# FFN input products of a two-block FP32 kernel as Strassen's seven block products, with the sums of weight blocks on GpSimd

## The chip, the cores and the metric

The kernel runs on one core of one Trainium2 chip. The metric is the device time of one launch in microseconds. Matrix products run on TensorE (PE in the profile; PEld is its weight load), the rest on VectorE (DVE), ScalarE (ACT) and GpSimd (POOL); SyncE (SP) issues the loads.

## The reference, cut to what matters

512 tokens of width 1024 pass a first block (gated linear attention, then an FFN) and a second one (FFN, pool and retention mixer, FFN), all in float32. The three FFNs have the width 2816 and are what the change touches:

```python
def swiglu_2(x, w1, w3, w2):
    return (jax.nn.silu(x @ w1) * (x @ w3)) @ w2
...
    h = h + 0.5 * swiglu_2(rmsnorm(h, ffn1_norm[l]), ffn1_w1[l], ffn1_w3[l], ffn1_w2[l])
```

`x @ w1` is called the gate here, `x @ w3` the up product, their gated product the hidden values (22 chunks of 128).

## The kernel before, in words

Activations are feature-major: a tile `[128, k, 512]` holds 128 features by 512 tokens for each k. Every float32 operand of a large product is two parts, an upper one rounded to the matmul's type (`hi`) and the rest (`lo`), and `mm3` makes three matmuls of each product: hi by hi, hi by lo, lo by hi. Each loads its own weights.

SP loads weights in units of 1 MB (1024 features by 256 columns) into `w_raw[0]` and `w_raw[1]`. ACT rounds a unit to `w_hi` (L1265), DVE subtracts it from the raw one into `w_lo` (L1712, one instruction of 2048 elements), and PE uses both. The FFN's first stage is `group`: a unit of gate columns into banks 0 and 1, a unit of up columns into banks 2 and 3, 96 matmuls of 512 tokens. ACT takes silu of the gate, DVE multiplies gate and up and splits the hidden value at once into `g_hi` and `g_lo` (L2282 or L2292, and L2297). 11 groups make an FFN's first stage; the first is written apart, ten are a loop. FFN 1 and 2 multiply their results by the norm's roots on DVE (`scaled`); FFN 0 does not. The second stage, `out_body`, runs over four column units in four parts each (`OUT_PARTS`).

Engines are in order, each with its own instruction list, and meet by semaphores alone; the order is written by hand. GpSimd has root computations (L420), sums of squares (L434, L436), residual adds (L458) and the pool mixer.

## Time and profile before

| | us |
|---|---|
| median of 3 runs | 1609.38 (1608.78 to 1611.98) |
| span of the profiled execution | 1607.1 |
| PE busy | 1596.4 |
| DVE busy | 849.0 |
| ACT busy | 502.5 |
| POOL busy | 119.9 |

The profiled execution has no own time beside its span: the profile gives the span from the first instruction to the last, and the median of the runs is 2.3 us above it. Busy is the union of an engine's instructions; matmuls overlap in their pipeline, so PE's pace is read from the distance of their starts.

### The profile page before, as it was taken

Reading aid. Unit: us, or ns where it says so; the run is one execution under the profiler, and the core shown is the slowest. Engines: PE = TensorE matmul, PEld = TensorE weight load, DVE = VectorE, ACT = ScalarE, POOL = GpSimd, SP = SyncE. Lnnn points to the kernel's source line nnn. Section 1 sums busy time; section 2 is a strip of 40 time slices with the busy share of each in tenths; the row PEclk is TensorE's granted clock in tenths of the full one; section 3 lists DMA queues with packets and bytes.
Section 4 is the critical chain, followed back from the end, with each engine's and each line's share of the span. In section 5 each row is a group of like instructions: output and inputs, shape, how many; then the busy total and the mean of one; then the engine's idle time right before and its main releaser. Section 6 shows DMA issues by size and latency. Waiting matters only on the chain.

```text
span 1607.1 us, 19314 instructions
## 1 busy us (share of the span) xinstructions
PE 1596.4 (99%) x7785; PEld 1343.6 (84%) x7785; DVE 849.0 (53%) x1050; ACT 502.5 (31%) x589; POOL 119.9 (7%) x106
## 2 busy tenths in 40 slices
PE   9999999999999999999999999999999999999998
PEld 7888888888888888888888888888988888888887
DVE  5898764664433344584454444346456544444444
ACT  4554375522222233442222223221323222222222
POOL 0100000020000000000000003135006000000000
PEclk9999999999999999999999999999999999999999
DMA  9544511222222123322222223342212322222332
GB/s 388 193 156 159 208 53 53 80 79 96 87 104 104 66 89 98 116 79 105 99 84 104 91 73 105 98 146 103 80 53 79 105 104 94 89 104 69 95 100 77
DMA packets 30647, 171.35 MB, mean 107 GB/s; under 512 B 3200, under 2 KB 5504, under 8 KB 17152
## 3 DMA queue, kind: packets, MB, share of 16 engines
q1 hardware_dynamic: 26240, 153.80, 27.4%
q0 software_dynamic: 4352, 16.78, 3.1%
q8 instruction: 39, 0.64, 0.2%
q14 instruction: 16, 0.13, 0.0%
HBM read 168.47 MB, written 2.10 MB: 106 GB/s over the span
## 4 chain that ended last, share of the span: by engine, by line
PE 99%; issue 0%; DVE 0%; POOL 0%; ACT 0%; POOLq 0%; DVEq 0%
PE bank L515 98%; PE bank L814 0%; PE bank L870 0%; POOL root L420 0%; PE bank L738 0%; PE bank L1143 0%; DVE y_ffn L2534 0%; ACT tmp L1500 0%; POOLq L123 0%; DVE qd L2111 0%; DVE kd L2111 0%; DVE tmp L2091 0%; DVE y_ffn L2532 0%; ACT mod_rows L1289 0%; DVEq L123 0%
## 5 line engine op out<-in xcount | busy, mean ns | idle before, releaser
L515 PE MATMUL bank<-a_hi,w_all 128*128 128x512 f32 x2490 | 764.7, 390 | 0.0
L515 PEld LDWEIGHTS bank<-a_hi,w_all 128*128 128x128 f32 x2490 | 466.5, 188 | 98.8 <-issue 2.5
L1712 DVE TENSOR_TENSOR w_all<-w_raw,w_all 128x2048 fp32r<-128x2048 f32 x140 | 323.3, 2309 | 360.5 <-ACT w_all L1265 360.3
L515 PE MATMUL bank<-a_lo,w_all 128*128 128x512 f32 x1245 | 477.1, 389 | 0.0
L1265 ACT ACTIVATE w_all<-w_raw 128x2048 fp32r<-128x2048 f32 x142 | 271.7, 1913 | 562.7 <-PE bank L515 562.7
L515 PE MATMUL bank<-g_hi,w_all 128*128 128x512 f32 (+1 forms) x1088 | 331.9, 386 | 0.0
L515 PEld LDWEIGHTS bank<-a_lo,w_all 128*128 128x128 f32 x1245 | 233.7, 188 | 48.8 <-issue 0.5
L515 PEld LDWEIGHTS bank<-g_hi,w_all 128*128 128x128 f32 x1088 | 203.9, 189 | 41.2
L515 PE MATMUL bank<-g_lo,w_all 128*128 128x512 f32 (+1 forms) x544 | 210.2, 386 | 0.0
L515 PEld LDWEIGHTS bank<-g_lo,w_all 128*128 128x128 f32 x544 | 102.5, 188 | 20.6
L515 PE MATMUL bank<-w_all,a_hi 128*128 128x512 f32 (+1 forms) x384 | 108.9, 359 | 0.0
L420 POOL TENSOR_TENSOR root<-col,power 128x4 f32<-128x4 f32 (+2 forms) x15 | 17.3, 1155 | 994.6 <-DVE col L1739 807.9
L1563 ACT ACTIVATE tmp<-tmp 128x512 f32<-128x512 f32 x44 | 27.7, 632 | 175.9 <-DVE tmp L2266 175.9
L2272 DVE TENSOR_TENSOR tmp<-bank,roots 128x512 f32<-128x512 f32 x44 | 30.3, 691 | 98.9 <-PE bank L515 98.9
L515 PE MATMUL bank<-w_all,a_lo 128*128 128x256 f32 (+1 forms) x256 | 78.9, 308 | 0.0
L515 PEld LDWEIGHTS bank<-w_all,a_hi 128*128 128x128 f32 x384 | 67.7, 189 | 10.1
L2266 DVE TENSOR_TENSOR tmp<-bank,roots 128x512 f32<-128x512 f32 x43 | 29.5, 688 | 87.7 <-PE bank L515 84.8
L515 PEld LDWEIGHTS bank<-w_all,a_lo 128*128 128x128 f32 x256 | 48.5, 189 | 2.7
L434 POOL TENSOR_TENSOR ke<-xT 128x512 f32 (+1 forms) x16 | 21.3, 1334 | 354.6 <-DVE xT L2229 353.0
L1733 DVE SCALAR_TENSOR_TENSOR mod_sum<-mod_raw,sc,mod_sum 128x512 f32<-128x512 f32 x56 | 42.1, 752 | 5.5 <-DMA mod_raw<-in_mod 3.1
L2297 DVE TENSOR_TENSOR g_lo<-tmp,g_hi 128x512 f32 (+1 forms) x66 | 42.5, 686 | 0.0
L2280 DVE TENSOR_TENSOR tmp<-tmp,bank 128x512 f32<-128x512 f32 x22 | 15.1, 688 | 49.7 <-PE bank L515 49.7
(289 smaller groups left out, 1339.3 us busy)
## 6 DMA issues: line engine op xcount, KB each, us to landing
w_raw<-in_ffn_in SPq DMA_DIRECT2D x66, 1024.0 KB, 4.8
w_raw<-in_ffn_out SPq DMA_DIRECT2D x24, 768.0 KB, 4.2
mod_raw<-in_mod POOLq DMA_DIRECT2D x16, 1024.0 KB, 5.6
w_raw<-in_ffn_out SPq DMA_DIRECT2D x24, 640.0 KB, 3.9
w_raw<-in_gla_in SPq DMA_DIRECT2D x10, 1024.0 KB, 5.1
w_raw<-in_mix_in SPq DMA_DIRECT2D x10, 1024.0 KB, 4.7
mod_w<-in_mod SPq DMA_DIRECT2D x8, 1024.0 KB, 18.4
w_raw<-in_gla_out SPq DMA_DIRECT2D x4, 1024.0 KB, 4.7
```

The source lines that it names most:

```text
L420: nc.gpsimd.tensor_tensor(root4[:, c0:c0 + n], col4[:, c0:c0 + n], power[:, 0:n], ALU.pow).then_inc(root_done, 1)
L434: nc.gpsimd.tensor_tensor(sq_pool[:], at, at, ALU.mult).then_inc(pool_squared, 1)
L515: return pe.matmul(out, lhs, rhs, start=first, stop=last, skip_group_check=True)
L1265: nc.scalar.activation(flat(w_hi[s]), flat(w_raw[s]), ACT.Copy).then_inc(hi_done[s], 1)
L1563: nc.scalar.activation(tmp[c][:], tmp[c][:], ACT.Silu).then_inc(silu_done, 1)
L1712: V.tensor_tensor(flat(w_lo[s]), flat(w_raw[s]), flat(w_hi[s]).bitcast(F32), ALU.subtract).then_inc(lo_done[s], 1)
L1733: V.scalar_tensor_tensor(total, w, x, total, ALU.mult, ALU.add).then_inc(done, 1)
L2266: V.tensor_tensor(tmp[c][:], gate, roots[:], ALU.mult).then_inc(gate_scaled, 1)
L2272: V.tensor_tensor(tmp[2 + c][:], bank[2 + c][:], roots[:], ALU.mult).then_inc(up_scaled, 1)
L2280: V.tensor_tensor(tmp[2 + c][:], tmp[c][:], bank[2 + c][:], ALU.mult).then_inc(prod_done, 1)
L2297: V.tensor_tensor(hidden(g_lo, m0, c), tmp[2 + c][:], hidden(g_hi, m0, c).bitcast(F32), ALU.subtract).then_inc(gated, 1)
```

## The change

Groups 1 to 10 of each FFN's first stage become `body`. The weight of a body is seen as a 2 by 2 block matrix for each half s of its columns (128 wide): gate or up by the first or second 512 features, `a11`, `a12` (gate), `a21`, `a22` (up). The activations are split by features and by token halves (256 tokens). Seven products of 4 feature chunks replace the eight blocks, for each s: 14 products of 12 matmuls with 256 tokens, 168 matmuls. The weights of four products are sums of blocks, s1 to s4, made on GpSimd (`block_sums`), and the activations of four are sums t1 to t4 (`token_operands` on GpSimd, two on DVE). Each operand is split into a ring of seven places (ACT upper, DVE lower, 512 elements each). Parts are copied from PSUM by ACT and added by DVE into halves of gate and up; in FFN 1 and 2 the up half is multiplied by the roots on GpSimd (`up_scale`). Hidden values stay float32 in `hid` and are split into `g_hi`, `g_lo` as the output stage begins. Group 0 stays as it was. Semaphores were merged; their waits are unchanged in place.

```diff
+OPERANDS = (("a11", 0), ("a12", 0), ("a11", 1), ("s2", 0), ("a12", 1), ("s2", 1), ("s1", 0),
+            ("s3", 0), ("s1", 1), ("s3", 1), ("a22", 0), ("s4", 0), ("a22", 1), ("s4", 1))
...
+SUM_ORDER = (("s1", 0), ("s2", 0), ("s1", 1), ("s2", 1), ("s3", 0), ("s3", 1), ("s4", 0), ("s4", 1))
...
+            def block_sums(name, s, first):
+                j = SUM_ORDER.index((name, s))
+                raw = [raw_block(s, b) for b in range(4)]
+                x, y, op = {"s1": (raw[2], raw[3], ALU.add), "s2": (sum_block("s1", s), raw[0], ALU.subtract),
+                            "s3": (raw[0], raw[2], ALU.subtract), "s4": (raw[1], sum_block("s2", s), ALU.subtract)}[name]
+                if name in ("s1", "s2") and s == 0:
+                    pool.wait_ge(pair_loaded[name == "s1"], cnt.off(pair_loaded[name == "s1"], 16))
+                if not first:
+                    pool.wait_ge(block_lo, cnt.off(block_lo, OPERANDS.index((name, s)) + 1 - STEPS))
+                if name == "s4":
+                    pool.wait_ge(block_lo, cnt.off(block_lo, OPERANDS.index(("a12", s)) + 1))
+                if name in ("s2", "s4"):
+                    pool.wait_ge(block_sum, cnt.off(block_sum, SUM_ORDER.index((("s1", "s2")[name == "s4"], s)) + 1))
+                nc.gpsimd.tensor_tensor(sum_block(name, s), x, y, op).then_inc(block_sum, 1)
+            def up_scale(s):
+                pool.wait_ge(parts_copied, cnt.off(parts_copied, s - 1))
+                pool.wait_ge(halves_summed, cnt.off(halves_summed, s - 3))
+                nc.gpsimd.tensor_tensor(tmp[2 + s][:], tmp[2 + s][:], roots[:], ALU.mult).then_inc(up_scaled, 1)
+            def token_operands(lows, between=None):
+                for k in range(KD):
+                    pool.wait_ge(norm_lo, lows + k + 1)
+                    nc.gpsimd.tensor_tensor(a_both[:, k], a_hi[:, k].bitcast(F32), a_lo[:, k].bitcast(F32), ALU.add).then_inc(joined, 1)
+                    cnt.expect(joined)
+                    if k == QK - 1:
+                        pool.wait_ge(joined, cnt.now(joined))
+                        nc.gpsimd.tensor_tensor(t_sum[0][:], a_both[:, 0:QK, TC:T], a_both[:, 0:QK, 0:TC], ALU.subtract).then_inc(joined, 1)
+                        cnt.expect(joined)
+                if between is not None:
+                    between()
+                pool.wait_ge(joined, cnt.now(joined))
+                nc.gpsimd.tensor_tensor(t_sum[1][:], a_both[:, QK:KD, TC:T], t_sum[0][:], ALU.subtract).then_inc(joined, 1)
+                cnt.expect(joined)
+            def ffn_sums(scaled=True):
```

PE's wait ahead of product 4, the output stage's new wait for each split hidden value, and DVE's sums and order in a body:

```diff
+                    product(3, r1x, "t2", False)
+                    pe.wait_ge(halves_summed, cnt.off(halves_summed, 1))
+                    product(4, r2, "b21", True, 1)
...
+                                    if begins and j == 0 and c == 0:
+                                        pe.wait_ge(operand_lo, cnt.next(operand_lo))
...
+                def hidden_lower(k):
+                    dve.wait_ge(operand_hi, cnt.next(operand_hi))
+                    V.tensor_tensor(g_lo[:, k], hid[:, k], g_hi[:, k].bitcast(F32), ALU.subtract).then_inc(operand_lo, 1)
...
+                def first_half(s):
+                    dve.wait_ge(gated, cnt.now(gated))
+                    dve.wait_ge(block_used, cnt.off(block_used, (2, 5)[s]))
+                    dve.wait_ge(parts_copied, cnt.off(parts_copied, 1 + s))
+                    V.tensor_tensor(part_of(tmp[s], 0), part_of(m1, s), part_of(bank[SECOND_BANK], s), ALU.add).then_inc(halves_summed, 1)
+                def up_half(s):
+                    dve.wait_ge(parts_copied, cnt.off(parts_copied, 5 + s))
+                    V.tensor_tensor(part_of(tmp[2 + s], 1), part_of(u3, s), part_of(bank[THIRD_BANKS[s]], 0), ALU.add).then_inc(halves_summed, 1)
+                def second_half(s, back):
+                    dve.wait_ge(block_used, cnt.off(block_used, (12, 14)[s] - (STEPS if back else 0)))
+                    V.tensor_tensor(part_of(tmp[s], 1), part_of(u2, s), part_of(bank[THIRD_BANKS[s]], 0), ALU.add).then_inc(halves_summed, 1)
+                    if scaled:
+                        dve.wait_ge(halves_summed, cnt.off(halves_summed, 5 + s - (6 if back else 0)))
+                        V.tensor_tensor(tmp[s][:], tmp[s][:], roots[:], ALU.mult).then_inc(gate_scaled, 1)
+                def hidden(m0, s):
+                    dve.wait_ge(silu_done, cnt.off(silu_done, s - 1))
+                    if scaled:
+                        dve.wait_ge(up_scaled, cnt.off(up_scaled, s - 1))
+                    else:
+                        dve.wait_ge(parts_copied, cnt.off(parts_copied, s - 1))
+                        dve.wait_ge(halves_summed, cnt.off(halves_summed, s - 3))
+                    to = hid[:, m0 + s] if isinstance(m0, int) else hid[:, bass.ds(m0 + s, 1)].rearrange("p o t -> p (o t)")
+                    V.tensor_tensor(to, tmp[s][:], tmp[2 + s][:], ALU.mult).then_inc(gated, 1)
+                    cnt.expect(gated)
+                def body(before=None, ends=False):
...
+                    lower(5)
+                    if before is not None:
+                        second_half(1, 2)
+                        hidden(before, 0)
+                    lower(6)
+                    lower(7)
+                    first_half(0)
+                    if before is not None:
+                        hidden(before, 1)
+                    lower(8)
+                    lower(9)
+                    lower(10)
+                    first_half(1)
+                    lower(11)
+                    lower(12)
+                    lower(13)
+                    up_half(0)
+                    ahead(14)
+                    ahead(15)
+                    up_half(1)
```

The order of DVE where FFN 0 begins (`a_lo` is the norm's lower part), before:

```order
L2171 SCALAR_TENSOR_TENSOR a_lo<-bank,mod,a_hi 128x512 [waits norm_hi_done] x2
L1712 TENSOR_TENSOR w_all<-w_raw_49,w_all 128x2048 [waits weight_hi_done0]
L2280 TENSOR_TENSOR tmp_135<-tmp_133,bank 128x512 [waits silu_done,ffn_up_ready]
L2282 TENSOR_TENSOR g_hi<-tmp_133,bank 128x512
L2280 TENSOR_TENSOR tmp_136<-tmp_134,bank 128x512 [waits silu_done,ffn_up_ready]
L2282 TENSOR_TENSOR g_hi<-tmp_134,bank 128x512
L2297 TENSOR_TENSOR g_lo<-tmp_135,g_hi 128x512 [waits gated_hi_done,product_done]
L2297 TENSOR_TENSOR g_lo<-tmp_136,g_hi 128x512 [waits gated_hi_done,product_done]
L2337 MEMSET qd_140 128x256 x2
```

and of the changed kernel:

```order
L2504 SCALAR_TENSOR_TENSOR a_lo<-bank,mod,a_hi 128x512 [waits norm_hi_done] x2
L2616 TENSOR_TENSOR t_sum_68<-a_both 128x1024 [waits operand_joined]
L2579 TENSOR_TENSOR ring<-w_raw_49,ring 128x512 [waits block_hi_done] x3
L2584 TENSOR_TENSOR t_lo_74<-t_sum_66,t_hi_70 128x1024 [waits operand_hi_done]
L2621 TENSOR_TENSOR t_sum_69<-a_both,t_sum_67 128x1024 [waits operand_joined]
L2584 TENSOR_TENSOR t_lo_75<-t_sum_67,t_hi_71 128x1024 [waits operand_hi_done]
L2579 TENSOR_TENSOR ring<-w_sum_78,ring 128x512 [waits block_hi_done]
L2631 TENSOR_TENSOR hid<-tmp_152,bank 128x512 [waits silu_done,ffn_up_ready]
L2631 TENSOR_TENSOR hid<-tmp_153,bank 128x512 [waits silu_done,ffn_up_ready]
L2579 TENSOR_TENSOR ring<-w_raw_49,ring 128x512 [waits block_hi_done]
L2584 TENSOR_TENSOR t_lo_76<-t_sum_68,t_hi_72 128x1024 [waits operand_hi_done]
L2584 TENSOR_TENSOR t_lo_77<-t_sum_69,t_hi_73 128x1024 [waits operand_hi_done]
```

The rows after `a_lo` are new: a token sum that waits for GpSimd stands first, and the ring's first lower parts and the lower parts of the four token sums (`t_lo`) follow. Behind them come lower parts 5, 6 and 7 and the first sum of halves, as `body` has them.

GpSimd at the same place, before:

```order
L458 TENSOR_TENSOR xT<-xT,y_gla 128x512 [waits y_scaled] x7
L420 TENSOR_TENSOR root_138<-col_137,power 128x4 [waits mean_square_done] x2
L111 UNCONDITIONAL_BRANCH
L111 ISA
L430 ISA [waits chunk_done]
```

and of the changed kernel:

```order
L614 TENSOR_TENSOR xT<-xT,y_gla 128x512 [waits y_scaled] x7
L577 TENSOR_TENSOR a_both<-a_hi,a_lo 128x512 [waits norm_lo_done] x4
L581 TENSOR_TENSOR t_sum_66<-a_both 128x1024 [waits operand_joined]
L577 TENSOR_TENSOR a_both<-a_hi,a_lo 128x512 [waits norm_lo_done] x4
L586 TENSOR_TENSOR t_sum_67<-a_both,t_sum_66 128x1024 [waits operand_joined]
L565 TENSOR_TENSOR w_sum_78<-w_raw_50 128x512 [waits weights_in_place1_loaded]
L565 TENSOR_TENSOR w_sum_78<-w_sum_78,w_raw_49 128x512 [waits block_sum_done,weights_in_place0_loaded]
L565 TENSOR_TENSOR w_sum_79<-w_raw_50 128x512
L565 TENSOR_TENSOR w_sum_79<-w_sum_79,w_raw_49 128x512 [waits block_sum_done]
L565 TENSOR_TENSOR w_sum_78<-w_raw_49,w_raw_50 128x512
L565 TENSOR_TENSOR w_sum_80<-w_raw_49,w_raw_50 128x512
L565 TENSOR_TENSOR w_sum_78<-w_raw_49,w_sum_78 128x512 [waits block_sum_done,block_lo_done]
```

Ten token operations and eight block sums (seven of them here) have come in between the residual adds and the roots of the second stage.

GpSimd in the loop of FFN 1 (`tmp_154`, `tmp_155` are the up halves, `w_sum` the block sums), where nothing stood before:

```order
L570 ISA [waits product_parts_copied]
L571 TENSOR_TENSOR tmp_154<-tmp_154,roots 128x512 [waits halves_summed]
L560 REGISTER_ALU
L565 TENSOR_TENSOR w_sum_78<-w_raw_49,w_raw_50 128x512 [waits block_lo_done]
L560 REGISTER_ALU
L565 TENSOR_TENSOR w_sum_80<-w_raw_49,w_raw_50 128x512 [waits block_lo_done]
L569 REGISTER_ALU
L570 REGISTER_ALU [waits product_parts_copied]
L571 TENSOR_TENSOR tmp_155<-tmp_155,roots 128x512 [waits halves_summed]
L560 REGISTER_ALU
L562 REGISTER_ALU [waits block_lo_done]
L564 REGISTER_ALU [waits block_lo_done]
```

The two scalings stand among the block sums, each behind a wait for the previous body's parts.

## Rows read from the trace of the kernel before

**Rows 1.** The page's head and its first part: busy us of each engine.

```profile
span 1607.1 us, 19314 instructions
PE 1596.4 (99%) x7785; PEld 1343.6 (84%) x7785; DVE 849.0 (53%) x1050; ACT 502.5 (31%) x589; POOL 119.9 (7%) x106
```

**Rows 2.** The page's part 4, the chain that ended last, by engine.

```profile
PE 99%; issue 0%; DVE 0%; POOL 0%; ACT 0%; POOLq 0%; DVEq 0%
```

**Rows 3.** A stretch of FFN 0's loop: width, busy (count) by engine, PEclk, DMA, GB/s.

```profile
400.00:500.00 100.00, 100.00 (x443) 82.81 (x442) 36.66 (x35) 22.07 (x18) 0.00 (x0) 1.00 0.28 102
```

**Rows 4.** Timeline of PE, first and last of 32 rows: start us, us, operation.

```profile
62.10 0.28 PE L515 MATMUL bank<-hc_lo,w_all 128*128 128x256 f32 x1
...
73.26 0.28 PE L515 MATMUL bank<-hc_lo,w_all 128*128 128x256 f32 x1
```

**Rows 5.** Groups by line and shape on DVE and ACT: busy us, mean ns.

```profile
L2297 DVE TENSOR_TENSOR g_lo<-tmp,g_hi 128x512 f32 x60 | 38.6, 686 | 0.0
...
L2046 DVE TENSOR_TENSOR sr<-sr,bank 128x256 f32<-128x256 f32 x16 | 6.1, 417 | 8.8 <-ACT sr L1459 8.8
...
L2119 DVE TENSOR_TENSOR w_all<-w_raw,w_all 128x1024 fp32r<-128x1024 f32 x4 | 4.8, 1220 | 0.7 <-ACT w_all L1265 0.7
...
L1563 ACT ACTIVATE tmp<-tmp 128x512 f32<-128x512 f32 x44 | 27.7, 632 | 175.9 <-DVE tmp L2266 175.9
```

**Rows 6.** Groups on POOL, the same view.

```profile
L436 POOL TENSOR_TENSOR qd<-qd,ke 128x512 f32<-128x512 f32 x16 | 30.3, 1896 | 1.3
```

**Rows 7.** Timeline of DVE and POOL where FFN 1 ends.

```profile
965.04 1.30 POOL L436 TENSOR_TENSOR qd<-qd,ke 128x512 f32<-128x512 f32 x1
965.60 0.69 DVE L2229 SCALAR_TENSOR_TENSOR xT<-bank,xT 128x512 f32<-128x512 f32 x1 [1.96 <-PE bank L515]
...
967.55 2.29 DVE L1712 TENSOR_TENSOR w_all<-w_raw,w_all 128x2048 fp32r<-128x2048 f32 x1 [1.26 <-ACT w_all L1265]
967.67 3.32 POOL L436 TENSOR_TENSOR qd<-qd,ke 128x512 f32<-128x512 f32 x1
```

**Rows 8.** The same, before FFN 2, POOL first.

```profile
1209.90 1.29 POOL L436 TENSOR_TENSOR qd<-qd,ke 128x512 f32<-128x512 f32 x1
...
1210.57 2.78 DVE L1712 TENSOR_TENSOR w_all<-w_raw,w_all 128x2048 fp32r<-128x2048 f32 x1 [1.26 <-ACT w_all L1265]
```

**Rows 9.** DVE, two lower parts of hidden values back to back, FFN 0.

```profile
352.27 1.29 DVE L2297 TENSOR_TENSOR g_lo<-tmp,g_hi 128x512 fp32r<-128x512 f32 x2
```

**Rows 10.** Beginning of FFN 0: last residual add, last norm parts, first matmul after group 0.

```profile
337.62 1.30 POOL L458 TENSOR_TENSOR xT<-xT,y_gla 128x512 f32<-128x512 f32 x1 [0.62 <-DVE y_gla L2150]
...
339.63 1.60 DVE L2171 SCALAR_TENSOR_TENSOR a_lo<-bank,mod,a_hi 128x512 fp32r<-128x512 f32 x2
...
349.90 0.39 PE L515 MATMUL bank<-a_hi,w_all 128*128 128x512 f32 x1
```

**Rows 11.** Beginnings of FFN 1 (last norm parts) and FFN 2 (root, broadcast).

```profile
708.78 1.62 DVE L2200 SCALAR_TENSOR_TENSOR a_lo<-xT,cols,a_hi 128x512 fp32r<-128x512 f32 x2
...
1247.72 1.02 POOL L420 TENSOR_TENSOR root<-col,power 128x4 f32<-128x4 f32 x1 [5.93 <-DVE col L1739]
...
1252.85 1.02 PE L515 MATMUL bank<-tmp,ones 128*128 128x512 f32 x2
```

**Rows 12.** The page's part 6: count, KB each, median us to landing.

```profile
w_raw<-in_ffn_in SPq DMA_DIRECT2D x66, 1024.0 KB, 4.8
```

**Rows 13.** PE as FFN 1 begins: the window's granted clock, then its timeline.

```profile
690.00:700.00 10.00, 9.92 (x49) 8.47 (x50) 9.31 (x18) 3.19 (x4) 2.03 (x2) 0.83 0.29 105
...
691.00 1.03 PE L515 MATMUL bank<-ones,ke 128*128 128x1 f32 x8
...
694.34 0.63 PE L515 MATMUL bank<-g_lo,w_all 128*128 128x512 f32 x1
694.77 1.05 PE L515 MATMUL bank<-g_hi,w_all 128*128 128x512 f32 x2
```

More of the change, by code:

```diff
@@ L92, in now, with off @@
         value = self.n.get(sem, 0) - back
+        assert value > 0, str(sem)
+        if self.i is not None and self.per.get(sem, 0):
+            value = self.i * self.per[sem] + value
+        return value
+    def off(self, sem, by):
+        value = self.n.get(sem, 0) + by
         assert value > 0, str(sem)
@@ L150, in build @@
         w_raw = [place(f"w_raw{s}", [P, KD, UC]) for s in range(2)]
+        ring = place("ring", [P, RING, 2, QK, P], F32R, top[0])
+        late = place("late", [P, QK, UC], F32, top[0] + 28 * KB)
         w_all = place("w_all", [P, 2, 2, KD, UC], F32R)
@@ new lines, in ffn @@
+                for s in range(2):
+                    load(s, w_in[s])
+                for s in range(2):
+                    sp.wait_ge(hi_done[s], cnt.next(hi_done[s]))
+                    sp.wait_ge(lo_done[s], cnt.next(lo_done[s]))
+                    sp.dma_start(flat(w_raw[s]), w_in[2 + s]).then_inc(pair_loaded[s], 16)
+                sp.wait_ge(up_ready, cnt.next(up_ready, CPU))
+                load_late(w_in[3, :, UNIT // 2:])
+                cnt.expect(block_sum, SUMS)
+                cnt.expect(block_lo, STEPS)
@@ L391, in _ @@
+                load_out(0, True)
+                with cnt.loop(D // UC - 1, {x: 2 for x in both}) as i:
+                    load_out(i + 1)
             ffn(a["ffn0_in"], a["ffn0_out"])
@@ L415, in _ @@
             cnt = Counts(pool)
+            for x in pair_loaded:
+                cnt.expect(x, 16)
             pool.wait_ge(const_set, 3)
@@ new lines, in ffn_sums, with body @@
+            def ffn_sums(scaled=True):
+                def body(first=False):
+                    for name, s in SUM_ORDER:
+                        if not first and scaled and s == 0 and name in ("s3", "s4"):
+                            up_scale(name == "s4")
+                        block_sums(name, s, first)
+                    cnt.expect(block_sum, SUMS)
+                    cnt.expect(block_lo, STEPS)
+                    cnt.expect(parts_copied, 8)
+                    cnt.expect(halves_summed, 6)
+                    for s in range(2):
+                        cnt.expect(pair_loaded[s], 16)
+                body(True)
+                with cnt.loop(BODIES - 1, {block_sum: SUMS, block_lo: STEPS, parts_copied: 8, halves_summed: 6,
+                                           pair_loaded[0]: 16, pair_loaded[1]: 16}):
+                    body()
+                if scaled:
+                    up_scale(0)
+                    up_scale(1)
@@ L1570, in group @@
-                    act.wait_ge(up_ready, cnt.next(up_ready, CPU))
-                    if not scaled:
-                        cnt.expect(gated, CPU)
+                        token_upper(0)
+                    for j in range(3):
+                        upper(j, True)
+                    token_upper(1)
+                    upper(3, True)
+                    act.wait_ge(up_ready, cnt.next(up_ready, CPU))
+                    upper(4, True)
+                    token_upper(2)
+                    upper(5, True)
@@ new lines, in end @@
+                def end():
+                    hidden_upper(2)
+                    hidden_upper(3)
+                    silu(1, 2)
+                    hidden_upper(4)
+                    hidden_upper(5)
+                    act.wait_ge(block_used, cnt.off(block_used, 0))
+                    split_hi(1)
+                    for k in range(6, 12):
+                        hidden_upper(k)
+                    act.wait_ge(unit_used[0], cnt.next(unit_used[0]))
+                    split_hi(0)
+                    for k in range(12, KF):
+                        hidden_upper(k)
@@ new lines, in body, with ahead @@
+                def body(before=None, ends=False):
+                    def ahead(j):
+                        if not ends:
+                            lower(j)
+                    lower(5)
[18 more added lines that the diff above has]
+                    up_half(1)
+                    ahead(16)
+                    ahead(17)
+                    if ends:
+                        split_lo(0)
+                    second_half(0, 0)
+                    if ends:
+                        for k in range(2):
+                            hidden_lower(k)
+                    ahead(18)
+                    for x, more in ((block_hi, STEPS), (block_used, STEPS), (parts_copied, 8), (halves_summed, 6), (silu_done, 2), *(((up_scaled, 2), (gate_scaled, 2)) if scaled else ())):
+                        cnt.expect(x, more)
@@ L2300, in out_body @@
                 def out_body(i, final=False):
                     for j in range(2):
-                        split_lo(1)
+                        begins = i == 0 and j == 0
+                        if not begins:
+                            split_lo(1)
                         p = 2 * i + j - 1
```

488 lines of the change are left out of this document (340 added, 148 removed).

## Prediction, made before the changed kernel ran

> **What bounds the kernel now.** The page's first part comes first: TensorE is busy 1596.4 of 1607.1 us [rows 1]. The chain of waits that ended last says the same: 99% of it is PE [rows 2]. So PE's pace is the kernel's time, and nothing that DVE, ACT or POOL save is worth anything; what they add costs nothing until PE waits for it. Then the pace: in a stretch of the FFN loop 443 matmuls of 512 tokens start in 100 us, 225.7 ns each [rows 3]. A group has 96, that is 21.67 us. For matmuls of 256 tokens the timeline has a stretch where each also loads its own weights: 32 rows of one kind, every third matmul, from 62.10 to 73.26 us: 11.16 us / 93 = 120 ns [rows 4]. Half the tokens is not half the time; each matmul carries some 13 ns of its own.
>
> **PE's share of the change.** A body has 168 matmuls at 120 ns = 20.16 us (one product of 12: 1.44 us) in place of 21.67. Seven eighths of the work gives back 7%, 1.51 us a body. With 30 bodies: -45 us. That is all that PE can win.
>
> The Trainium skill (TensorE: Matmul & The Clock Gate, Back-to-back issue gap) gives N/2.4 + 2.5 ns, an estimate of 109 and 216 ns. By it the saving were 96 x 215.8 - 168 x 109.2 = 2.4 us a body, 71 us in all. The rows have 120 and 225.7 ns, so they decide.
>
> **What the others get.** Per body DVE makes 14 lower parts of 512 elements, 2 hidden values and in FFN 1 and 2 two gate scalings, all with both inputs in SBUF (686 ns each, 0.60 from start to start [rows 5, 9]), and six sums of 256 with one input in PSUM (417 ns [rows 5]): 18 x 0.6 + 6 x 0.4 = 13.2 us. ACT: 14 upper parts and 2 silus at 0.63 us [rows 5] and eight short copies, which I take at 0.4 like DVE's: 13.3 us. POOL: 8 block sums, and 2 scalings in FFN 1 and 2. Alone each would fit under 20.16 us.
>
> But POOL and DVE don't run side by side. A DVE instruction with two SBUF inputs starts at 967.55; POOL's add, issued 0.12 us later, takes 3.32 us [rows 7] instead of 1.29 [rows 8]: it waited 2.03 us, to 0.15 before DVE's end. The other way round, DVE's 2.29 us become 2.78 when POOL was first, and it begins at 1211.06, 0.13 before POOL's end [rows 8]. The mean of 16 such adds is 1896 ns [rows 6]. A DVE instruction with one input in PSUM isn't hindered (0.69 us under an add of 1.30 [rows 7]). So each pair excludes the other: a POOL add for 1.29 - 0.13 = 1.16 us, a DVE instruction for its length less 0.15, 0.54 us for 512 elements. With both queues full they alternate, 1.70 us a pair.
>
> In FFN 1 and 2 this gives 10 x 1.16 + 18 x 0.54 = 21.3 us a body, more than PE's 20.16 and just under the old 21.67. In FFN 0 it is 8 x 1.16 + 16 x 0.54 = 17.9 us, which fits.
>
> The Trainium skill (SBUF — State Buffer, Who interferes with whom) speaks against the change: the one that issues second fully blocks. The same page (SBUF: two separate sides) has the pair held for the whole instruction. Held to the end of every instruction, 10 x 1.29 + 18 x 0.69 would be 25.3 us a body; the rows show a release 0.13 to 0.15 us before it, so I go by 21.3.
>
> **Loop of FFN 1 and 2.** Where does the wait fall? Product 4 waits for the first sum of halves, and ahead of that DVE's order has gate scaling 1, hidden 0 and lower parts 6 and 7; the chain starts when product 13 of the body before is done, and PE has four products, 5.76 us, until then. Alone DVE needs 0.6 + 0.4 + 0.7 + 4 x 0.6, with waits some 4.5 us: hidden. But POOL's up scaling waits for product 10, done 4.3 us before a body ends, and a copy. From 3.8 us before the end POOL has six instructions ready (scaling, s3, s3, scaling, s4, s4), and DVE six with two SBUF inputs up to hidden 0 (lower part 17, gate scaling 0, lower parts 18 and 19, gate scaling 1, hidden 0). Alternating, 6 x 1.70 = 10.2 us, up to 6.4 us into the next body; two lower parts and the sum add 1.8: 8.2 against 5.76, a stall of 2.45 us and a body of 22.6 us. Weights are no second bound: from s4 to the next load's landing 4.8 us [rows 12] plus four adds is far below that. Bounds: 0 (the two queues miss each other) to 5 us (six more DVE instructions meet an add of 1.16 us each). I take 2.45, nearest to rows 7 and 8. Nine bodies in each of two FFNs: +44. FFN 0's POOL has no scalings and meets DVE less: 0.3 us x 9 = +3.
>
> **Beginnings.** Here the long chain is new. In FFN 0 POOL's last residual add ends at 338.92, and group 0 on PE ends at 349.90 [rows 10]. POOL then has eight joins (1.16 us of the port and some 0.05 between two: 1.21) and the first token sum of 1024 elements (2.4 us): 338.9 + 9.7 + 2.4, with the waits 351.3. DVE waits for that ahead of the first lower part of the ring, so PE stands from 349.9. Up to product 4 DVE has six instructions of 1024 elements on token sums (1220 ns each [rows 5], 1.15 from start to start), eight lower parts, two hidden values and the sum: 6.9 + 4.8 + 1.2 + 0.4 = 13.3 us, from 351.4 to 364.7 (the second token sum of POOL is done in time). PE could have been there after four products, at 355.7: 9 us lost with nothing contended. With POOL's own eight block sums and second token sum in between (9.3 + 2.3 us, less 1.2 under the hidden values, which read PSUM) it is 375: 19 us. In FFN 1 the norm's parts end at 710.4 [rows 11] and POOL's joins stretch them besides; the same count gives 6 to 18. In FFN 2 the root stands behind eight joins, so it slips from 1247.7 by 7 us or more, and the broadcast that PE makes in its own order at 1252.85 [rows 11] slips too: 7 to 18. Sum 22 to 55; I take 16 each, +48, nearer the top since all eight block sums are queued there.
>
> **Ends.** The first output chunks wait for the last hidden values and their lower parts on DVE; chunk 4 is due 2.7 us after product 13, and the chain (sum, scaling, silu, hidden, lower parts) takes 4.5: 1.8 x 3 = +5 (0 to 12). The other splits run ahead: 22 x 0.6 us and three weight splits of 1.7 against 30 us of PE.
>
> **Clock.** After PE did one-column matmuls at 691.00 the granted clock of that 10 us stretch is 0.83, and a matmul takes 0.43 us from start to start (694.34 to 694.77) [rows 13]: 1.2 GHz, the lower level. A mean of 0.83 over 10 us is 3.4 us at that level, 1.7 us lost. I expect that once per beginning, where PE stands for several us: 1.7 x 3 = +5 (0 to 15).
>
> **Sum.** -45 + 44 + 3 + 48 + 5 + 5 = +60. On the span, 1607.1 + 60 = 1667; the median of the runs lies 2.3 us above the span: 1669.
>
> **Rivals.**
> The port is shared but the loop hides it: the queues settle so that POOL works in PE's products 5 to 12, and only beginnings and ends cost. For it: 21.3 us leaves room within 22.6; against: POOL's scalings come late by their waits. -45 + 48 + 5 + 5 + some 5 = +18: 1627.
>
> Faster. The beginnings too find POOL early, and DVE isn't held: -45 + 22 + 5 + 5 = -13: 1596. The mechanism is PE's shorter bodies alone; it wins if the stall ahead of product 4 stays under 0.6 us in loops and the beginnings under 9. For it: 1.51 us of PE is sure. Against: rows 7 and 8.
>
> The clock falls in loops: if 2.45 us of standing each body is enough for the lower level, 18 x 1.7 = +31 on top: 1700. For it: rows 13; against: the array is busy for 89% of a body.
>
> The port held to the last nanosecond: a body of 25.3 us, 18 x 2.7 more, +49, 1718. Against it stands the early release in rows 7 and 8. It is the Trainium skill's rule of above (SBUF — State Buffer) taken by its letter.
>
> That the change doesn't do what it says I leave out: the order of PE is written out, 14 products of 12 matmuls a body.
>
> **How the numbers follow.** Forecast 58% (own range 1640 to 1692), loop hides it 14%, faster 13%, clock in loops 9%, whole lock 3%, the rest between. The range 1610 to 1706 leaves out the faster case and the lock. Faster by over 0.2% 0.13, within 0.2% (3.2 us, what a measurement here can tell from none) 0.03, slower 0.84.
>
> **What would show it.** PE matmuls of 256 tokens 0.12 us apart; POOL adds with means of 1.5 to 1.9 us and DVE lower parts well over 0.69; waits of PE for DVE's sums of halves (a line of the PSUM sum) of 2 to 3 us in each loop body of FFN 1 and 2, almost none in FFN 0's; PE idle 10 us or more as each FFN's first body starts. Wrong would be: PE still at 99%, or adds at 1.3 us beside a full DVE.

## The result, and the profile after

The changed kernel takes 1722.84 us (median of 4 runs, 1721.34 to 1724.98), the kernel before beside it 1610.25: ratio 1.0697 [1.0682, 1.0712], 7% slower. The forecast was 1669 us with a range to 1706. The sign was right, the size was half of what came: the profiled execution's span grew by 116.1 us, not by 60. All ratios here are of undisturbed executions; one of the four of experiment 4 ran at a mean granted clock of 0.554 (2583 us) and is left out of its ratio.

The page's head and its rows on busy time and granted clock, then its chain of waits. They answer to [rows 1, 2].

```profile
span 1723.2 us, 27275 instructions
PE 1600.6 (93%) x9945; PEld 1448.2 (84%) x9945; DVE 1252.9 (73%) x1502; ACT 754.9 (44%) x1267; POOL 618.6 (36%) x416
PEclk9999999979999999888999999999999999999999
PE 18%; DVE 1%; ACT 1%; issue 1%; POOL 0%; POOLq 0%; DVEq 0%; ACTq 0%
```

The 18% is a share of the span, and this chain could be followed back only to 1349.55 us: all its rows add up to 21%, the last 374 us. So it can't be held against the 99% before; within those 374 us PE has 85%. What has changed is PE's idle time: 99% busy before, 93% now. Its busy time didn't fall by the 45 us that the arithmetic saves either. One reason is the clock, whose mean over the span is 0.960, and 0.997 before: three slices of the clock row, 689 to 818 us, from the beginning of FFN 1 into its loop, read 8. The view of PE's waits by releaser says who is late (engine, tile, line waited for: us in total, times, longest):

```profile
PE bank L677 <- DVE tmp L2648: 62.2, 21, 6.6
PE bank L677 <- DVE qd L2722: 18.6, 3, 6.9
PE bank L677 <- DVE ring L2579: 16.6, 4, 5.6
PE bank L677 <- DVE tmp L2075: 7.5, 1, 7.5
```

L2648 is the first sum of halves: 18 loop bodies and three first bodies. L2722 is the zeroing of the square sums ahead of each output stage, which the forecast doesn't have at all. The kernel before made it behind group 0 (L2337 in its order of DVE, the last row there). The changed kernel keeps copied parts (`m1`) in the same tile during the bodies, and makes the zeroing behind the last hidden value: not all waits stayed in place.

**Loops.** Windows of the changed kernel: FFN 0's loop over the stretch of [rows 3], then two bodies of FFN 1 (columns as there), the longest of the 18 and one at full clock, and PE's timeline where product 4 of the first of them starts.

```profile
400.00:500.00 100.00, 100.00 (x836) 100.00 (x835) 95.61 (x111) 60.15 (x120) 60.55 (x40) 1.00 0.38 131
807.51:833.16 25.65, 23.11 (x168) 22.91 (x169) 20.98 (x25) 11.78 (x24) 15.73 (x11) 0.88 0.29 101
930.63:953.58 22.95, 20.41 (x168) 20.21 (x169) 22.26 (x25) 11.78 (x24) 16.12 (x11) 1.00 0.34 115
...
807.51 0.58 PE L677 MATMUL bank<-a_hi,ring 128*128 128x256 f32 x1 [2.54 <-DVE tmp L2648]
807.88 0.42 PE L677 MATMUL bank<-a_lo,ring 128*128 128x256 f32 x1
808.10 0.63 PE L677 MATMUL bank<-a_hi,ring 128*128 128x256 f32 x2
```

836 matmuls in 100 us are about 119.6 ns each; by the starts of product 4, 20.16 us apart for 168 matmuls, it is 120.0, as forecast. FFN 0's loop never waits. In FFN 1 and 2 PE waits 2.54 us ahead of each product 4. Behind the wait at 807.51 the matmuls start 0.22 us apart, not 0.12: the granted clock of the body is 0.88, and this pace is the lower of the two levels, 1.2 GHz. Product 4 comes every (978.03 - 758.35) / 9 = 24.41 us in FFN 1 and 24.12 in FFN 2, 24.27 in the mean. Three of these 18 bodies, that at 930.63 among them, take 22.95 us at a granted clock of 1.00, behind the same wait of 2.54 us.

The same view of DVE, then of POOL, ahead of that wait. They answer to [rows 7, 8].

```profile
798.95 1.78 DVE L2579 TENSOR_TENSOR ring<-w_raw,ring 128x512 fp32r<-128x512 f32 x1
800.65 1.78 DVE L2579 TENSOR_TENSOR ring<-w_sum,ring 128x512 fp32r<-128x512 f32 x1
802.35 0.41 DVE L2658 TENSOR_TENSOR tmp<-kd,bank 128x256 f32<-128x256 f32 x1
...
804.06 1.78 DVE L2672 TENSOR_TENSOR hid<-tmp,tmp 128x512 f32 x1
```

```profile
796.72 3.46 POOL L565 TENSOR_TENSOR w_sum<-w_raw,w_raw 128x512 f32<-128x512 f32 x2
800.14 1.75 POOL L571 TENSOR_TENSOR tmp<-tmp,roots 128x512 f32<-128x512 f32 x1
```

The two alternate, 1.70 us a pair, as forecast: a lower part that took 0.69 us alone takes 1.78, and starts 1.70 after the one ahead. The instruction with a PSUM input (L2658) takes 0.41 in between.

**Beginning of FFN 1.** The window ahead of product 4, then three rows of DVE in it:

```profile
735.76:758.22 22.46, 10.63 (x61) 9.03 (x59) 22.46 (x21) 10.46 (x19) 14.57 (x9) 0.79 0.33 117
...
735.76 1.72 DVE L2616 TENSOR_TENSOR t_sum<-a_both 128x1024 f32<-128x1024 f32 x1
742.49 2.30 DVE L2584 TENSOR_TENSOR t_lo<-t_sum,t_hi 128x1024 fp32r<-128x1024 f32 x1
757.89 0.41 DVE L2648 TENSOR_TENSOR tmp<-qd,bank 128x256 f32<-128x256 f32 x1
```

DVE is busy 22.46 of 22.46 us while PE has work for half of it. A token lower part of 1.22 us alone takes 2.30.

**End of FFN 0.** DVE's last rows, and PE's first of the output stage:

```profile
577.71 0.68 DVE L2672 TENSOR_TENSOR hid<-tmp,tmp 128x512 f32<-128x512 f32 x1
578.39 0.55 DVE L2722 MEMSET qd<- 128x256 f32 x2
...
578.72 0.79 PE L677 MATMUL bank<-g_hi,w_all 128*128 128x512 f32 x1 [4.83 <-DVE qd L2722]
```

The first output chunk needs early hidden values only, but PE also waits for the zeroing, and DVE makes it behind the last hidden value. In FFN 1 and 2 this wait is 6.90 us.

**Where the 116 us are**, by the first matmul of each stage and the starts of product 4 in the two traces. In the kernel before, ten groups take 217.6 us (349.90 to 567.50), 21.76 each, not 21.67: the 443 matmuls of [rows 3] include those that lie across the edges of the stretch. So a body saves 1.60 us.

| Part | Forecast | Measured |
|---|---|---|
| PE's shorter bodies, 30 | -45 | -48 (30 x 1.60) |
| Loops of FFN 1 and 2, over 20.16 us a body | +44 | +73.9 (18 x 4.10) |
| Loop of FFN 0 | +3 | +2.0 (all of it between the first two products 4: 22.11 us at a clock of 0.90, no wait) |
| Three beginnings, clock included | +53 | +60.4 (19.0, 22.0, 19.4) |
| Three ends | +5 | +20.6 (5.0, 8.4, 7.1) |
| Head, output stages, mixer | 0 | +7.3 |

The parts add up to 116.2.

### The profile page after: what moved, and what is told of

It reads as the page before. It is cut to its first block and busy times, and to the rows that moved or that the text cites. A ratio compares the mean times of both kernels' runs of the same rounds, so it can differ in the third digit from the quotient of the medians.

```text
span 1723.2 us, 27275 instructions
## 1 busy us (share of the span) xinstructions
PE 1600.6 (93%) x9945; PEld 1448.2 (84%) x9945; DVE 1252.9 (73%) x1502; ACT 754.9 (44%) x1267; POOL 618.6 (36%) x416
## 5 line engine op out<-in xcount | busy, mean ns | idle before, releaser
L677 PE MATMUL bank<-t_hi,ring 128*128 128x256 f32 x1920 | 370.6, 288 | 12.6 <-DVE ring L2579 10.1
L677 PE MATMUL bank<-a_hi,ring 128*128 128x256 f32 x1440 | 297.9, 299 | 68.6 <-DVE tmp L2648 62.2
L677 PEld LDWEIGHTS bank<-t_hi,ring 128*128 128x128 f32 x1920 | 315.8, 198 | 13.1 <-DVE t_lo L2584 8.4
L677 PEld LDWEIGHTS bank<-a_hi,ring 128*128 128x128 f32 x1440 | 248.0, 205 | 74.1 <-DVE ring L2579 49.5
L677 PE MATMUL bank<-t_lo,ring 128*128 128x256 f32 x960 | 276.3, 288 | 0.0
L2579 DVE TENSOR_TENSOR ring<-w_sum,ring 128x512 fp32r<-128x512 f32 x240 | 252.5, 1069 | 30.1 <-ACT ring L1781 29.2
L677 PE MATMUL bank<-a_lo,ring 128*128 128x256 f32 x720 | 213.4, 296 | 0.0
L677 PEld LDWEIGHTS bank<-t_lo,ring 128*128 128x128 f32 x960 | 190.1, 198 | 0.0
L677 PE MATMUL bank<-a_hi,w_all 128*128 128x512 f32 x570 | 176.0, 399 | 0.0
L677 PEld LDWEIGHTS bank<-a_hi,w_all 128*128 128x128 f32 x570 | 107.6, 191 | 25.1 <-issue 2.8
```

Of the source, the lines that this page charges most:

```text
L677: return pe.matmul(out, lhs, rhs, start=first, stop=last, skip_group_check=True)
L2579: V.tensor_tensor(ring_block(j, 1), operand(j), ring_block(j, 0).bitcast(F32), ALU.subtract).then_inc(block_lo, 1)
```

## The experiments

Each is an edit of the changed kernel. Lines that begin with + or - are against it.

**1. Matmuls on constants in the wait (e1_fill).** Does the lower clock cost time, or is it hidden?

```diff
+                    if scaled and not first:
+                        keep_busy(7, 20)
                     pe.wait_ge(halves_summed, cnt.off(halves_summed, 1))
                     product(4, r2, "b21", True, 1)
```

> In the loops of FFN 1 and 2, PE makes 20 matmuls of 128 columns on constants (0.12 us each, 2.4 us) into an unused bank ahead of its wait before product 4; all else as changed. Theory 'the clock falls because PE stands': the wait before product 4 shrinks from 2.54 us by what the fill takes, the granted clock stays at 1.0 in the loops, a loop body is 20.16 + 2.7 = 22.9 us where it was 24.3, and 18 bodies give 25 us: 1698. Rival 'the port and the chain are all of it, the lower clock lies in the shadow of waits': body unchanged at 24.3, 1723. A second rival: the fill delays product 4, since the stall is not steady: 1730.

1737.44 us, ratio 1.0787 [1.0768, 1.0806]: slower than every theory had it. PE's timeline tells why: each of the 20 is two matmuls in the trace, so the fill took 4.38 us where 2.54 were free.

```profile
806.66 4.62 PE L677 MATMUL bank<-ones 128*128 128x128 f32 x40
811.04 0.37 PE L677 MATMUL bank<-a_hi,ring 128*128 128x256 f32 x1
```

But the body, 24.62 us, is the 4.38 us of fill and 20.24 us of products: no matmul at half pace. So the size was mended:

**2. The fill cut to the wait (e7_short_fill)**, `keep_busy(7, 12)` in the same place.

> The changed kernel with 24 matmuls of 128 columns on constants, 0.109 us each = 2.6 us, put ahead of the wait for the first sum of halves in each loop body of FFN 1 and 2, where PE stood for 2.54 us. In the run with 40 of them (4.4 us) each body took 20.24 + 4.38 = 24.62 us with no matmul at half pace, so 1.8 us a body were only the fill's own excess. Theory C (the stall alone costs 2.54 us a body and the rest, 1.5 us a body, is the lower clock that follows a stand): bodies of 22.9 us, 18 x 1.4 = 25 us less than the changed kernel: 1698. Rival (the DVE and POOL queues set the period, and PE's lower clock is hidden in it): about 1723 to 1725.

1702.27 us, 1.0574 [1.0556, 1.0591]: 20.6 us under the changed kernel, by adding work and removing none. One body, and PE at its start:

```profile
1387.69:1410.64 22.95, 22.95 (x194) 22.90 (x193) 22.35 (x25) 11.79 (x24) 16.11 (x11) 1.00 0.33 114
...
1384.98 2.84 PE L677 MATMUL bank<-ones 128*128 128x128 f32 x24
1387.69 0.38 PE L677 MATMUL bank<-a_hi,ring 128*128 128x256 f32 x1
```

The period is 22.95 us at full clock against 24.27. So 2.79 us of each body are the wait, 18 x 2.79 = 50 us, and the other 23.7 of the loops' 73.9 us come with the lower clock: 1.32 us a body in the mean, none in three. The fill won back 19.5 of them between the first and the last product 4 of FFN 1 and 2. The other 4 lie between the first two products 4 of each (24.49 and 25.45 us), behind the wait of the first bodies, which have no fill.

**3. The sum of halves first (e3_order).** Is the wait the order on DVE, or its load?

```diff
-                    lower(5)
                     if before is not None:
                         second_half(1, 2)
                         hidden(before, 0)
+                    first_half(0)
+                    lower(5)
                     lower(6)
...
                     lower(7)
-                    first_half(0)
...
```

> DVE's order in a body is changed: second half sum 1, gate scaling 1, hidden 0, then the first sum of halves, and only then lower parts 5, 6 and 7. Theory 'the first sum of halves is late because three lower parts stand ahead of it, at up to 1.70 us each': the sum is ready about 5.2 us into a body, before PE's product 3 ends at 5.76, no wait and no fall of the clock; bodies go to 21.3 (the port's sum) or a little more: 18 x 3.0 = 54 us or up to 70: 1650 to 1669. Rival 'the port's capacity is the bound': the wait moves to another product and a body stays at 23 us or more: 1700 or more.

1702.03 us, 1.0575 [1.0552, 1.0598]. One body of FFN 1, and the three places where PE waits in it:

```profile
807.94:831.07 23.13, 20.91 (x169) 20.32 (x169) 22.84 (x25) 11.63 (x25) 16.44 (x10) 1.00 0.33 116
...
807.94 0.38 PE L677 MATMUL bank<-a_hi,ring 128*128 128x256 f32 x1 [1.27 <-DVE tmp L2648]
818.72 0.38 PE L677 MATMUL bank<-a_hi,ring 128*128 128x256 f32 x1 [0.44 <-DVE tmp L2653]
828.10 0.38 PE L677 MATMUL bank<-t_hi,ring 128*128 128x256 f32 x1 [0.50 <-ACT qd L1794]
```

The 20.8 us saved look like the chain's share. They aren't: the steady period, 23.12 us, is no shorter than that of experiment 2, which left the order alone. The wait was cut into three short ones, behind which the granted clock stays at 1.00, and DVE has 22.84 of 23.13 us busy. What the order won is the clock; the load stays. That theory, the chain as the cause, fell here. In FFN 0 the same order cost 0.9 us a body (21.10 in place of 20.16, also in experiment 7).

**4. GpSimd without its block sums (e2_small_sums).** After the first body of each FFN a sum is made of one column per chunk (the rest of these sums is left out).

```diff
+                out = sum_block(name, s)
+                if not first:
+                    out, x, y = out[:, :, 0:1], x[:, :, 0:1], y[:, :, 0:1]
-                nc.gpsimd.tensor_tensor(sum_block(name, s), x, y, op).then_inc(block_sum, 1)
+                nc.gpsimd.tensor_tensor(out, x, y, op).then_inc(block_sum, 1)
```

> After the first body of each FFN the eight block sums on GpSimd are made of one column in 128 only (4 elements a partition), with the same waits and signals; the other columns keep the first body's values. Theory 'DVE and GpSimd take turns at one port': without GpSimd's long adds the DVE's lower parts are back at 0.69 us, the chain up to product 4 fits under PE's four products, the wait of 2.54 us and with it the lower clock are gone, loop bodies are 20.2 us where they were 24.1 to 24.4: 18 x 4.1 = 74, about 1649. Rival 'the chain of hidden values is too long by itself' (its waits between ACT, DVE and PE): a wait of 2 us or more stays, 1700 to 1720.

The ratio is 1.0288 [1.0266, 1.0309], 1656.1 us; 1649 was expected.

```profile
807.94:828.20 20.26, 20.26 (x171) 20.26 (x170) 15.27 (x25) 12.08 (x25) 6.12 (x10) 1.00 0.39 130
```

DVE made the same 25 instructions in 15.27 us, not 22.26, and no body waits. Of the loops' 73.9 us, 69 go with GpSimd's adds; 4.8 stay between the first two products 4 of each FFN (22.63 and 22.51 us), behind the waits of the first bodies. The 47 us that stay over the kernel before are what beginnings, ends and the rest cost, less the 48 that PE's bodies give back.

**5. Up half scaled on DVE (e5_up_dve)**: that part of the change undone in the loops, the two scalings of a body moved from `up_scale` on GpSimd to

```diff
+                        V.tensor_tensor(tmp[2 + s][:], tmp[2 + s][:], roots[:], ALU.mult).then_inc(up_scaled, 1)
```

> The up half is scaled on DVE in the loops of FFN 1 and 2, not on GpSimd: 20 DVE instructions with two SBUF inputs a body in place of 18, and 8 POOL adds in place of 10. In the run with the sum of halves put first, DVE was never idle in a loop body of 23.12 us, so I now count the DVE queue by itself: its own instructions (0.60 us each, and 0.35 for each of the six with a PSUM input) and 1.05 to 1.16 us for each POOL instruction that it waits for. Theory Q (the DVE queue with POOL's time in it is the bound): 20 x 0.6 + 2.1 + 8 x 1.05 to 1.16 = 22.5 to 23.4 us a body, 0.9 to 1.8 less than the 24.27 of the changed kernel, so 1688 to 1706. Rival P (the port's own sum, as in the prediction, 8 x 1.16 + 20 x 0.54 = 20.1 us, and the late scalings on POOL are what makes the stall): bodies of 20.2 to 20.5, 1650 to 1655.

**6. Three moves, and small up scalings (e8_all_small_up).** The moves are those of experiment 7; on top of them, one column of the up half is scaled (the rest of that work is left out).

```diff
-                nc.gpsimd.tensor_tensor(tmp[2 + s][:], tmp[2 + s][:], roots[:], ALU.mult).then_inc(up_scaled, 1)
+                nc.gpsimd.tensor_tensor(tmp[2 + s][:, 0:1], tmp[2 + s][:, 0:1], roots[:, 0:1], ALU.mult).then_inc(up_scaled, 1)
```

> The three moves of the run before the last in this list, and GpSimd's two up scalings in each loop body cut to one column of 512 (the up half stays unscaled in the rest: that work is left out). Theory Q (DVE's queue with POOL's time in it): 18 x 0.6 + 2.1 + 8 x 1.05 to 1.16 = 21.3 to 22.2 us a body against 23.1 to 23.2: 16 to 33 us under the kernel with the three moves, so 1645 to 1662. Rival P (the port's own sum): 8 x 1.16 + 18 x 0.54 = 19.0 us, so PE's 20.2 is the bound, 52 us under: 1626.

Measured: 1688.35 us, 1.0486 [1.0469, 1.0504], and 1653.90 us, 1.0273 [1.0256, 1.0291]. Both times are inside theory Q's bounds and far from the port's own sum, but the periods, 22.38 and 21.07 us, are 0.1 and 0.2 under the lower bounds that it gave, and e8_all_small_up is 37.9 us under the kernel with the three moves where 16 to 33 were expected. A body of FFN 1 in each:

```profile
802.51:824.89 22.38, 20.65 (x169) 20.25 (x169) 22.12 (x27) 11.72 (x25) 13.03 (x9) 1.00 0.33 118
```

```profile
810.22:831.29 21.07, 20.62 (x169) 20.27 (x169) 20.78 (x25) 11.61 (x25) 13.74 (x10) 1.00 0.37 124
```

DVE has 99% of both busy. Three periods give two prices:

| Kernel | DVE instr. with two SBUF inputs | Full POOL instr. | Period, us |
|---|---|---|---|
| e3_order | 18 | 10 | 23.12 |
| e5_up_dve | 20 | 8 | 22.38 |
| e8_all_small_up | 18 | 8 | 21.07 |

If the periods are sums of these, two DVE instructions are 1.31 us, 0.65 each, and two POOL instructions are 2.05 us of DVE's time, 1.03 each. (The one-column scalings that stay in e8_all_small_up make the second a little low; the orders of the first and third are alike, that of the second is the changed kernel's.)

**7. The three moves (e6_all)**: the order of experiment 3; the zeroing of experiment 8; and in each first body

```diff
+                    for j in range(3):
+                        lower(j)
                     dve.wait_ge(joined, (KD + 2) * n + KD + 1)
                     V.tensor_tensor(t_sum[2][:], a_both[:, QK:KD, TC:T], a_both[:, 0:QK, TC:T], ALU.subtract).then_inc(t_late, 1)
-                    for j in range(3):
-                        lower(j)
```

with the last two token lower parts behind lower parts 6 and 7.

> Three moves on DVE together, no work left out: the first sum of halves before lower parts 5 to 7; the zeroing of the square sums before the last body's end; and where an FFN begins, the ring's first three lower parts ahead of the token sum that waits for GpSimd, and the last two token lower parts behind lower parts 6 and 7. If the three losses are separate, the gains add: 1722.8 - 20.8 (order) - 14.1 (zeroing) - 3 x 2.5 to 4 (beginnings: two instructions of 1.15 us and what POOL puts between them no longer stand ahead of product 4) = 1676 to 1680. Rival (the beginnings are bound by the whole of DVE's and POOL's work, which only moves): 1688.

1691.77 us, 1.0514 [1.0496, 1.0531]. 1676 to 1680 was expected. The first two moves alone give 1722.8 - 20.8 - 14.1 = 1687.9, so the third gave nothing. PE in FFN 0's first body, and the window of a later body there:

```profile
367.53 0.55 PE L677 MATMUL bank<-t_hi,ring 128*128 128x256 f32 x1 [11.35 <-ACT qd L1794]
```

```profile
406.00:427.10 21.10, 20.41 (x169) 20.21 (x168) 20.11 (x23) 12.06 (x24) 12.25 (x8) 1.00 0.34 125
```

Product 0 no longer waits, but product 3 starts at 367.53, where it had been 368.76: several waits became one of 11.35 us. Product 4 came earlier, but the next one 25.65 us behind it, in place of 22.11. The second row is the side effect of the order in FFN 0: 21.10 us a body in place of 20.2.

**8. The zeroing earlier (e4_zero_early).**

```diff
                     first_half(1)
+                    if ends:
+                        dve.wait_ge(halves_summed, cnt.off(halves_summed, 2))
+                        for j in range(2):
+                            V.memset(sq_sum[:, j * (T // 2):(j + 1) * (T // 2)], 0.0).then_inc(pair_out[j], 1)
+                            cnt.expect(pair_out[j])
                     lower(11)
```

and the same lines taken out behind the last hidden value.

> The two clearings of the sum of squares, whose signals release PE into the output stage, stand behind lower part 11 of the last body, not behind the last hidden value. Theory 'PE stands 4.8 to 6.9 us before each output stage only for these': it starts at once, meets a shorter wait at chunk 4 or 5 (the hidden chain), and 3 to 5 us a stage are gained, with less of the lower clock after it: 9 to 15 us, 1711. Rival 'the last hidden values' chain is the wait': it moves whole to chunk 2 to 4: 1720.

1708.69 us, 1.0619 [1.0597, 1.0642], 14.1 us less: as expected. From the last product 4 to the output stage the trace has 10.4 us less (3.5, 4.0, 2.9). The rest is not the ends': FFN 1's loop is 4.6 us shorter here, with three bodies at full clock where the changed kernel's trace has one. What is late next is the lower parts, 1.31 us in FFN 0 and 2.65 in FFN 1 and 2:

```profile
573.85 0.47 PE L677 MATMUL bank<-g_hi,w_all 128*128 128x512 f32 x1 [1.31 <-DVE g_lo L2589]
```

**9. First bodies without block sums (e13_first_memset).** GpSimd writes zeros in their place (those sums are left out).

```diff
+                if first:
+                    nc.gpsimd.memset(sum_block(name, s), 0.0).then_inc(block_sum, 1)
+                    return
```

> The changed kernel with GpSimd's eight block sums of each FFN's first body replaced by zeroing the same tiles (those sums are left out; loops and all waits as they were). In FFN 1's beginning DVE was busy 22.46 of the 22.46 us ahead of product 4. Its own instructions there are 6 x 1.15 (token sums and their lower parts) + 8 x 0.6 + 4 x 0.6 (two gate or up scalings, two hidden values) + 0.35 = 14.5 us; what is left, 8 us, is the eight block sums at 1.03 each. Theory Q (the beginning of an FFN too is DVE's queue with GpSimd's time in it): if a zeroing reads nothing and does not hold DVE up, 8 us less in FFN 1 and 2 each and up to 8 in FFN 0, so 1699 to 1707. Rival (the beginning is bound by the norm's parts, GpSimd's joins and the token sums, which all stay): at most 1 us each, 1720 to 1723. What a zeroing on GpSimd takes beside DVE no trace here shows: if it holds DVE as an add does, the time stays too, which the lengths of DVE's instructions would tell.

1698.59 us, 1.0552 [1.0525, 1.0580]: 24.3 us less, just under the bounds of 1699 to 1707. Counted from the stage ahead, the first product 4 comes 7.7 us earlier in FFN 0, 7.9 in FFN 1 and 4.7 in FFN 2, whose wait of 7.5 us for a POOL root's diagonal stays: 20.3 us. Part of the rest lies in the bodies behind it: in FFN 0 the next product 4 comes after 20.26 us in place of 22.11. DVE, then POOL, as FFN 1 begins:

```profile
724.40 1.21 DVE L2619 TENSOR_TENSOR t_sum<-a_both 128x1024 f32<-128x1024 f32 x1
725.70 1.90 DVE L2582 TENSOR_TENSOR ring<-w_raw,ring 128x512 fp32r<-128x512 f32 x3
...
738.60 0.41 DVE L2651 TENSOR_TENSOR tmp<-qd,bank 128x256 f32<-128x256 f32 x1
```

```profile
724.96 1.47 POOL L566 MEMSET w_sum<- 128x512 f32 x3
```

From the first token sum to the sum of halves DVE takes 738.60 - 724.40 = 14.2 us, where it had been 22.1. The token sum and the first lower part run beside zeroings, unhindered: 1.21 us, and 1.90 for three lower parts, 0.60 from start to start. The Trainium skill (SBUF — State Buffer, Who interferes with whom) says that a DVE instruction with two SBUF inputs contends with a GpSimd instruction that reads SBUF, not with one that only writes it; these rows agree.

**10. Combinations.** e10_up_dve_zero_early is experiments 5 and 8 together. e11_begin_fill puts `keep_busy` ahead of products 3 and 4 of the first bodies. e12_all_kept is both.

> Two edits that each made the changed kernel faster, together: the up half scaled on DVE (1688.4 alone) and the square sums' zeroing put before the last body's end (14.1 alone). Theory: they lie in different stages and add: 1674. Rival (the last body's DVE queue is then longer by the scaling, and takes the zeroing's gain back): 1680 to 1688.

> The changed kernel with matmuls on constants ahead of products 3 and 4 of each FFN's first body, sized a little under the time that PE stood there (1.7 to 4.4 us ahead of product 3, 4.2 us ahead of product 4). The work before product 4 is DVE's, so product 4 starts no earlier; what can change is the pace behind it. Theory: the stand ahead of product 4 costs 1.7 to 3.4 us of lower clock in each of three FFNs: 1713 to 1718. Rival (DVE's queue is behind PE in the whole first body, so PE's pace there is hidden): 1721 to 1725.

> The edits of the two runs above together: up half scaled on DVE, zeroing early, matmuls on constants in the first bodies. If all gains add, 1674 - 5 to 10 = 1664 to 1669; it is the best version with all the work that the runs so far point to, and should still be 3 to 4% slower than the kernel before, since three beginnings of about 18 us and 18 bodies of 22.4 us stay. Rival (the fills gain nothing): 1674.

1678.18 us, 1.0416 [1.0394, 1.0438]; 1719.14, 1.0679 [1.0654, 1.0705]; 1675.95, 1.0413 [1.0393, 1.0433]. The first two gains add but for 4 us. They came back in the output stages of FFN 1 and 2, 2.3 and 2.0 us longer than in experiment 8's trace: the second wait, 3.4 us behind the first in FFN 1, is followed by matmuls at the lower level of the clock (0.43 us from start to start; the granted clock from 972.61 to 985.60 is 0.74):

```profile
975.98 0.80 PE L672 MATMUL bank<-g_hi,w_all 128*128 128x512 f32 x1 [1.41 <-DVE g_lo L2584]
```

The fills in the beginnings moved the time by 3.7 and 2.2 us, and the intervals overlap, so the times are inconclusive. The traces say more: in FFN 0 the first two products 4 are 20.24 us apart with the fill, at a granted clock of 1.00, and 22.11 at 0.90 without it. So e10_up_dve_zero_early is 4 us over its forecast, e11_begin_fill 1 us over its own, and e12_all_kept ends by the rival's 1674. No version with all the work came near the kernel before; the best is 4% slower.

## Why the prediction was half right

Two steps failed: the clock, priced at nothing in the loops' bodies, where it took 23.7 us, and the ends, at +5 us where they took 20.6. The other misses, in the wait, the beginnings and the rest, are 6, 7 and 7 us.

**PE's part, right.** 120.0 ns a matmul, a body of 20.2 us, no wait in FFN 0's loop. The saving is 1.60 us a body, not 1.51: the group's 21.67 us came from a count that has the matmuls across the stretch's edges in it.

**The alternation at the port, right in mechanism.** 1.70 us a pair in the trace, and experiment 4 shows that 69 of the loops' 73.9 us hang on GpSimd's adds.

**The port's sum, 21.3 us a body: the wrong bound, though it decided little here.** I added the times for which the pair is held, and took the rest of DVE's work to run beside GpSimd. But DVE has one queue: what it waits at the port comes on top of its six instructions with a PSUM input. The bound is DVE's own time plus about 1.03 us for each GpSimd instruction. An estimate from experiment 6's prices: 18 x 0.65 + 10 x 1.03 = 22.0, and 1.1 us is left of the 23.12 for the PSUM ones. That they take so little because they hide part of an add is not shown. The forecast of the body, 22.6 us, came from another step, the chain ahead of product 4 with its stall of 2.45 us. Measured is 2.54 us of wait and 22.95 us of period at full clock. So +44 should have been 18 x 2.79 = +50. The chain was taken for the cause; experiment 3 shows that a shorter chain gives the same period.

**The clock in loops, wrong, and the largest miss of the loops.** The step "once per beginning" was priced +5, and the rival with 1.7 us a body got 9% because "the array is busy for 89% of a body". The runs put it at +23.7 us over the 18 bodies, 1.32 us a body in the mean; the fill of experiment 2 won back 19.5 of them. The Trainium skill (TensorE: Matmul & The Clock Gate, A second HAM failure mode: psum-queue depth-cycling) tells of a PE that stands briefly between groups of matmuls often enough for the clock to swing; the trace agrees (0.88 of full clock in the body at 807.51).

**The ends, wrong by 15.6 us.** The step looked at output chunk 4 and its chain. It missed that PE's output stage also waits for the zeroing of the square sums, which the change had moved behind the last hidden value in DVE's order, though its tile is free from the second sum of halves of the last body. Experiment 8 put it there: 10.4 us of it back.

**Beginnings, right in mechanism, a little low.** 53 forecast, 60.4 measured. FFN 1 and 2, with 22.0 and 19.4, lie above the 6 to 18 and 7 to 18 that I gave them. All eight block sums fall ahead of product 4, at 8 us of DVE's time in FFN 1 (experiment 9). The rest has GpSimd's token work in it, as forecast: beside its first token sum a norm part that takes 0.74 us alone takes 2.83, and PE waits 2.31 us for it. How much the joins cost in all no run separates.

```profile
720.59 2.68 POOL L581 TENSOR_TENSOR t_sum<-a_both 128x1024 f32<-128x1024 f32 x1
720.98 2.83 DVE L2533 SCALAR_TENSOR_TENSOR a_lo<-xT,cols,a_hi 128x512 fp32r<-128x512 f32 x1
```

**The rivals.** "Loop hides it" and "faster" fell. "The port held to the last nanosecond" (25.3 us a body) fell too: at full clock it is 23.1. "The clock falls in loops" was right in kind and a little dear, 31 us where 23.7 came; its 1700 lacks 15.6 us of the ends and 6 to 7 each of the wait, the beginnings and the rest.

**Left open.** The 7.3 us in head, output stages and mixer were not followed. What the clock costs in the beginnings is known for FFN 0 alone, 1.9 us behind its first product 4 (experiment 10), and only from single traces. Why three bodies keep the full clock behind the same wait is not known either.

## What to carry over

Where two engines exclude each other, count the whole queue of the one that others wait for: its own instructions, those that don't contend too, plus a full turn of the other engine for each of its instructions. Add a price for the clock to a stall that a loop repeats, even where PE is busy for nine tenths of the body; a fill of the stall's length tells it apart from the wait. When a chain's last link moves later, look for everything else that the waiting engine's semaphore covers: here a zeroing that could have been made earlier, which by its place alone cost 10 us.

## What the runs showed of the hardware

Unexpected was that added work can pay: 24 matmuls on constants in a stall of 2.54 us made the loop bodies 1.1 us shorter in the mean (24.27 to 23.18; 16 of the 18 take 22.95), as the granted clock stayed at 1.00. And that three waits of 1.27, 0.44 and 0.50 us in a body of 23.1 us left it at 1.00, where one of 2.54 us in each body left it there in three bodies of 18. GpSimd's zeroing of 512 elements takes 0.5 us and doesn't hold up a DVE instruction with two SBUF inputs; its add of the same size takes about 1.03 us of DVE's time, by the three periods of experiment 6.
